# Sharing a spectrum product between three engines: ScalarE copies each spectrum out of PSUM, GpSimd forms one of the four products from the copy

## The chip, the cores and the metric

One Trainium2 chip, of which the kernel uses one core with its engines TensorE (PE), VectorE (DVE), ScalarE (ACT), GpSimd (POOL) and the queue of SyncE (SP) for transfers. The metric is the time of one launch in device microseconds; the median of three runs is taken.

## What is computed

The reference is one inference step through two trunk layers of a hybrid model: layer 0 has windowed attention beside a Hyena convolution, layer 1 a gated DeltaNet beside neighbourhood attention, and each layer ends with an expert-choice SwiGLU network. The change is in the Hyena part of layer 0, for the 1024 sample tokens (the 128 prompt tokens go through the same stage and are not touched by it):

```python
def hyena_mixer(z, conv_w, conv_b, w1, b1, w2, b2, w3, freq, skip):
    ...
    v, x1, x2 = jnp.split(zf, 3, axis=-1)
    filt = hyena_filter_bank(L, w1, b1, w2, b2, w3, freq)
    ...
    def long_conv(u, o):
        y = jnp.fft.irfft(jnp.fft.rfft(u, n=2 * L, axis=1) * filt[None, :, o], n=2 * L, axis=1)[:, :L]
        return y + u * skip[o]

    y = x1 * long_conv(v, 0)
    y = x2 * long_conv(y, 1)
```

Each of 512 channels is convolved twice with a filter as long as the signal, in the frequency domain: a forward transform, a complex product with the filter's spectrum, an inverse transform.

## The kernel before

The program is a row of stages, each a `Stage` block with barriers at its ends; within a stage every engine has its own instruction list, and semaphores order them. The stage of the change is `hyena_signals`, called once, between the attention of layer 0 and its output projection. Nothing of a neighbouring stage overlaps it.

Work in it is cut into eight blocks, in this order: for each of the two convolution orders the sample's channels 0 to 255 and 256 to 511 (S0A, S0B, then S1A, S1B), each pair followed by the same halves of the prompt (P0A, P0B, P1A, P1B). A sample block has eight iterations (`ft`), one per pair of 128 frequencies and 128 channels; a prompt block has one. They are numbered through by `n`: 0 to 7 S0A, 8 to 15 S0B, 16 and 17 the prompt, 18 to 25 S1A, 26 to 33 S1B, 34 and 35 the prompt.

One sample iteration goes through these hands:

- TensorE, `forward` (L1629): eight matmuls, cosine and sine parts of two time phases, into one of two PSUM banks (`freq`). It waits until the products of iteration n - 2 have read that bank (`prod_done`).
- VectorE, `multiply` (L1743): four products of 128x512, the bank times four views of the filter's spectrum (`spec`, a ring of four buffers in SBUF, filled by SyncE's queue), into `prod`, a ring of two. `y` is the output's time phase, `k` real or imaginary; the two products of y = 1 come first. Then a sum over the input phases for y = 0 (L1748). The products of iteration n wait until GpSimd has finished iteration n - 2 (`y_done`).
- GpSimd: the same sum for y = 1 (L1813), which needs the first two products, then two operations that combine the sums into the spectrum `Y` (L1817), which need both sums.

After a block's eight iterations TensorE transforms back (`backward`, L1646), ScalarE takes the odd part out of PSUM with a scale (`take_odd`, L1695), and VectorE finishes each 128 channels with four operations (`convolve`: L1760 and L1761 from PSUM, L1763 and L1766 from SBUF, 1024 wide). VectorE also makes the even and odd parts of the next order's input (`fold`, L1725 and L1726, from SBUF alone), which TensorE turns (L1609) and ScalarE copies (L1686).

The order on each engine is written out by hand as a list of calls. TensorE runs, for instance, `forward(S0B, range(6, 8))`, then `backward(S0A, (0, 1))`, then the prompt's forward transforms, then `backward(S0B, (0,))`. So the inverse of S0A waits for the last forward transform of S0B, and that of S0B for `y_done` of all its iterations. SyncE's queue is in order too: the loads of the gate rows wait for `u_done` (L1766), and the spectrum loads behind them wait in line.

## Time and profile before

| what | value |
|---|---|
| median of three runs | 3908.98 us (3904.9 to 3911.44) |
| the profiled execution | 3899.8 us, its span 3898.0 us |
| busy in the whole span | PE 86%, DVE 60%, ACT 44%, POOL 17% |
| mean granted TensorE clock | 0.926 |
| products of this stage, first and last start | 730.6 to 885.8 us |

The span is the time from the first to the last instruction of the profiled execution; its own time has some 2 us around it. Busy shares are averages over very different stages, and the stage of the change is about a twentieth of the span, so only rows cut to that stage say what waits there. The page's chain of what ended last covers only the final norm, at the very end of the program, and does not reach back to this stage.

### The profile page before, as it was taken

Reading aid. Unit: us, or ns where it says so; the run is one execution under the profiler, and the core shown is the slowest. Engines: PE = TensorE matmul, PEld = TensorE weight load, DVE = VectorE, ACT = ScalarE, POOL = GpSimd, SP = SyncE. Lnnn points to the kernel's source line nnn. Section 1 sums busy time; section 2 is a strip of 40 time slices with the busy share of each in tenths; the row PEclk is TensorE's granted clock in tenths of the full one; section 3 lists DMA queues with packets and bytes.
Section 4 is the critical chain, followed back from the end, with each engine's and each line's share of the span. In section 5 each row is a group of like instructions: output and inputs, shape, how many; then the busy total and the mean of one; then the engine's idle time right before and its main releaser. Section 6 shows DMA issues by size and latency. Waiting matters only on the chain. (4 is left out here: it accounts for less than half of the span.)

```text
span 3898.0 us, 60341 instructions
## 1 busy us (share of the span) xinstructions
PE 3349.1 (86%) x24369; PEld 2499.5 (64%) x24369; DVE 2319.3 (60%) x3530; ACT 1731.1 (44%) x2640; POOL 663.9 (17%) x544
## 2 busy tenths in 40 slices
PE   5979969677869999999699965877869599999994
PEld 1459945466646666666599954656757366666663
DVE  5253333685578888887521443535663778788884
ACT  2131145212346556666311134657853365666653
POOL 0011041342100000000110001507831000110000
PEclk8989989888979999999899987988979799999997
DMA  4143187425448888888344238117444578888875
GB/s 174 81 155 98 57 272 232 135 92 176 160 172 289 288 293 292 291 288 287 127 132 126 74 115 287 30 45 235 141 151 141 186 288 291 294 289 284 282 280 203
DMA packets 364075, 763.50 MB, mean 196 GB/s; under 512 B 88616, under 2 KB 204888, under 8 KB 361609
## 3 DMA queue, kind: packets, MB, share of 16 engines
q1 hardware_dynamic: 343530, 699.73, 50.7%
q0 software_dynamic: 17648, 59.50, 6.3%
q8 instruction: 193, 3.16, 0.3%
q10 hardware_dynamic: 2618, 0.40, 0.1%
q14 instruction: 86, 0.70, 0.1%
HBM read 640.89 MB, written 119.29 MB: 195 GB/s over the span
## 5 line engine op out<-in xcount | busy, mean ns | idle before, releaser
L2599 DVE TENSOR_TENSOR moe_w_low<-ffn_w,moe_w_high 128x1024 fp32r<-128x1024 f32 x768 | 900.3, 1220 | 90.0 <-ACT moe_w_high L2524 83.5
L2524 ACT ACTIVATE moe_w_high<-ffn_w 128x1024 fp32r<-128x1024 f32 x768 | 780.5, 1054 | 202.8 <-DMA ffn_w<-moe_w_gate 115.1
L2450 PE MATMUL moe_small<-ffn_w,ffn_xpT 128*16 128x512 f32 x2048 | 238.3, 594 | 0.0
L2428 PE MATMUL moe_G<-moe_w_high,moe_xT_high 128*128 128x512 f32 x512 | 185.3, 443 | 17.0 <-DVE moe_xT_low L2562 10.3
L2376 POOL DMA_INDIRECT scratch_x<-moe_ys,keep_slot_s x32 | 50.6, 1581 | 865.0 <-DVE moe_ys L2591 865.0
L224 PE MATMUL proj_mm<-proj_hT_low,proj_w_high 128*128 128x384 f32 x576 | 193.2, 335 | 0.0
L224 PE MATMUL proj_mm<-proj_hT_high,proj_w_low 128*128 128x384 f32 x576 | 193.1, 335 | 0.0
L224 PE MATMUL proj_mm<-proj_hT_high,proj_w_high 128*128 128x384 f32 x576 | 193.1, 335 | 0.0
L224 PE MATMUL proj_mm<-proj_w_high,proj_hT_high 128*128 128x416 f32 (+1 forms) x504 | 178.1, 353 | 12.0 <-POOL proj_hT_low L344 8.3
L224 PE MATMUL proj_mm<-proj_w_high,proj_hT_low 128*128 128x416 f32 (+1 forms) x504 | 176.8, 351 | 0.0
L224 PE MATMUL proj_mm<-proj_w_low,proj_hT_high 128*128 128x416 f32 (+1 forms) x504 | 175.8, 349 | 0.0
L2428 PE MATMUL moe_Y<-moe_w_high,moe_hT_high 128*128 128x512 f32 x512 | 166.6, 407 | 0.0
L2552 DVE TENSOR_SCALAR moe_xT<-moe_turn,keep_coef 128x128 f32<-128x128 f32 x248 | 84.7, 404 | 135.1 <-PE moe_turn L2404 135.1
L2428 PE MATMUL moe_G<-moe_w_low,moe_xT_high 128*128 128x512 f32 x512 | 161.9, 398 | 0.0
L2428 PE MATMUL moe_U<-moe_w_high,moe_xT_high 128*128 128x512 f32 x512 | 160.2, 394 | 0.0
L2428 PE MATMUL moe_G<-moe_w_high,moe_xT_low 128*128 128x512 f32 x512 | 160.0, 394 | 0.0
L2428 PE MATMUL moe_U<-moe_w_low,moe_xT_high 128*128 128x512 f32 x512 | 159.7, 393 | 0.0
L2428 PE MATMUL moe_Y<-moe_w_low,moe_hT_high 128*128 128x512 f32 x512 | 159.4, 392 | 0.0
L2428 PE MATMUL moe_Y<-moe_w_high,moe_hT_low 128*128 128x512 f32 x512 | 158.7, 391 | 0.0
L2428 PE MATMUL moe_U<-moe_w_high,moe_xT_low 128*128 128x512 f32 x512 | 158.6, 391 | 0.0
L451 ACT ACTIVATE proj_z<-proj_mm 128x384 f32<-128x384 f32 (+1 forms) x96 | 37.0, 412 | 263.6 <-PE proj_mm L224 259.7
L466 DVE CAST proj_w_high<-proj_w_raw 128x768 fp32r<-128x768 f32 (+1 forms) x60 | 34.0, 567 | 200.7 <-PE proj_mm L224 157.0
(500 smaller groups left out, 7138.4 us busy)
## 6 DMA issues: line engine op xcount, KB each, us to landing
ffn_w<-moe_w_gate SPq DMA_DIRECT2D x256, 512.0 KB, 6.0
ffn_w<-moe_w_up SPq DMA_DIRECT2D x256, 512.0 KB, 6.9
ffn_w<-moe_w_down SPq DMA_DIRECT2D x256, 512.0 KB, 5.3
attnrun_m_w<-w_ada SPq DMA_DIRECT2D x40, 1024.0 KB
scratch_spec<-front_room SPq DMA_DIRECT2D x8, 1536.0 KB, 5.1
scratch_conv<-proj_zf POOLq DMA_DIRECT2D x24, 512.0 KB, 2.9
hyena_spec<-scratch_spec SPq DMA_DIRECT2D x32, 384.0 KB, 3.5
scratch_tm<-proj_tm SPq DMA_DIRECT2D x45, 208.0 KB, 2.0
```

Of the source, the lines that this page charges most:

```text
L224: mm = nc.tensor.matmul(out, lhs(a, k), rhs(b, k), start=first and n == 0, stop=last and n == len(passes) - 1)
L451: ins = nc.scalar.activation(z[c % 2][:, lo + to:hi + to], banks[n % 6][:, lo - g * TG:hi - g * TG], ACT.Copy)
L466: nc.vector.tensor_copy(high, raw).then_inc(w_up, 1)
L2376: nc.gpsimd.indirect_dma_start(out=io["x"][l], out_offset=bass.IndirectOffsetOnAxis(ap=rows, axis=0), in_=src[e % 2][:], in_offset=None, c ...
L2428: mm = nc.tensor.matmul(bank[:, half, :], stat[a][:, k, :], cut[b][:, half * BANK:(half + 1) * BANK], start=k == 0 and i == 0, stop=k == K ...
L2450: nc.tensor.matmul(out, stat, w, start=k == 0, stop=k == KD - 1, tile_position=(0, 32 * q)).then_inc(small_done, 1)
L2524: nc.scalar.activation(w_high[n % CUT_ROOM][:], raw_rows(wall, n), ACT.Copy).then_inc(w_up, 1)
L2552: ins = nc.vector.tensor_scalar(xT[:, k, :], turned(k, e), co[:, 0, k:k + 1], co[:, 1, k:k + 1], ALU.mult, ALU.add)
L2599: nc.vector.tensor_tensor(w_low[n % CUT_ROOM][:], raw_rows(wall, n), w_high[n % CUT_ROOM][:].bitcast(F32), ALU.subtract).then_inc(w_cut, 1)
```

## The change

In the sample's iterations the fourth product (y = 1, k = 1) moves from VectorE to GpSimd. GpSimd does not read the PSUM bank itself: ScalarE first copies the bank's 128x512 to `side`, a new ring of two buffers in SBUF. GpSimd then multiplies the copy with the spectrum ahead of its sum. New waits: ScalarE's copy waits for the transform (`dft_done`) and for the side buffer (`crossed`, two iterations back); VectorE's products wait for the copy (`copied`); GpSimd's product waits for the copy and for the spectrum's load, its sum for its own product; and the spectrum loads wait for GpSimd's product four iterations back as well. On ScalarE the copies stand in the list where TensorE's forward transforms stand in its own.

```diff
@@ -1486,6 +1486,7 @@
         bwd_p = s.sb("bwd_p", [P, 2, 64])
         spec = [s.sb(f"spec{i}", [P, 2 * 3 * P]) for i in range(SPECS)]
         prod = s.sb("prod", [P, 2, 2, 2, 2, 2, P])
+        side = [s.sb(f"side{i}", [P, 2, HC]) for i in range(2)]
         odd = s.sb("odd", [P, 2, TS // 2])
         conv = s.sb("conv", [P, TS])
         skip = s.sb("skip", [P, 2, NCH])
@@ -1494,7 +1495,7 @@
         time_banks = [s.ps(f"time{i}", [P, 2, BANK]) for i in range(2)]
         u_in = [[s.sem(f"u_in{i}{h}") for h in range(2)] for i in range(2)]
         fwd_in, fwd_p_in, bwd_in = [s.sem(f"fwd_in{f}") for f in range(4)], s.sem("fwd_p_in"), s.sem("bwd_in")
-        summed, odd_summed = s.sem("summed"), s.sem("odd_summed")
+        summed, odd_summed, copied, crossed = s.sem("summed"), s.sem("odd_summed"), s.sem("copied"), s.sem("crossed")
         spec_in = [s.sem(f"spec_in{i}") for i in range(SPECS)]
         gate_in = [s.sem(f"gate_in{i}") for i in range(2)]
         folded, turned, turn_taken, dft_done, prod_done, y_done, inv_done, odd_done, conv_done, u_done = (
@@ -1514,6 +1515,10 @@
 
             return sum(g.ft for g, _, _ in blocks[:b] if g.i == 0)
 
+        def copies(n):
+
+            return sum(1 for b, (g, _, _) in enumerate(blocks) for m in range(freq0[b], freq0[b + 1]) if g.i == 0 and m < n)
+
         def channels(b):
             return (2 * blocks[b][2], 2 * blocks[b][2] + 1)
 
@@ -1535,6 +1540,7 @@
                     n = freq0[b] + f
                     if n >= SPECS:
                         sp.wait_ge(prod_done, 2 * (n - SPECS + 1))
+                        sp.wait_ge(crossed, copies(n - SPECS + 1))
                     if g.i == 0:
                         sp.dma_start(spec[n % SPECS][:], io["spec"][f // 2, o, :, 2 * h + f % 2].rearrange("p s v c -> p (s v c)")).then_inc(spec_in[n % SPECS], 16)
                     else:
@@ -1685,6 +1691,15 @@
                     act.wait_ge(turned, n + 1)
                     nc.scalar.activation(eoT_of[g.i][0:g.rows, t, part, h * HC:(h + 1) * HC], turn_banks[n % 2][0:g.rows, 0:HC], ACT.Copy).then_inc(turn_taken, 1)
 
+            def copy(b, fs):
+                for f in fs:
+                    n = freq0[b] + f
+                    c = copies(n)
+                    act.wait_ge(dft_done, n + 1)
+                    if c >= 2:
+                        act.wait_ge(crossed, c - 1)
+                    nc.scalar.activation(side[c % 2][:], freq_banks[n % 2][:], ACT.Copy).then_inc(copied, 1)
+
             def take_odd(b, js):
                 g, o, _ = blocks[b]
                 for j in js:
@@ -1695,18 +1710,26 @@
                     nc.scalar.activation(odd[:, i % 2, 0:g.half], time_banks[i % 2][:, 1, 0:g.half], ACT.Copy, scale=keep.tap_scale[:, g.i, at:at + 1]).then_inc(odd_done, 1)
 
             take_turned(S0A)
+            copy(S0A, range(0, 6))
             take_turned(S0B)
+            copy(S0A, range(6, 8))
+            copy(S0B, range(0, 6))
             take_turned(P0A)
             take_turned(P0B)
+            copy(S0B, range(6, 8))
             take_odd(S0A, (0, 1))
             take_odd(S0B, (0,))
             take_turned(S1A)
             take_odd(S0B, (1,))
+            copy(S1A, range(0, 6))
             take_turned(S1B)
+            copy(S1A, range(6, 8))
             take_odd(P0A, (0, 1))
             take_odd(P0B, (0, 1))
+            copy(S1B, range(0, 6))
             take_turned(P1A)
             take_turned(P1B)
+            copy(S1B, range(6, 8))
             for b in (S1A, S1B, P1A, P1B):
                 take_odd(b, (0, 1))
 
@@ -1730,6 +1753,7 @@
                 for f in fs:
                     n = freq0[b] + f
                     dve.wait_ge(dft_done, n + 1)
+                    dve.wait_ge(copied, copies(n + 1))
                     dve.wait_ge(spec_in[n % SPECS], 16 * (n // SPECS + 1))
                     if n >= 2:
                         dve.wait_ge(y_done, 2 * (n - 1))
@@ -1739,7 +1763,7 @@
                             nc.vector.tensor_tensor(both(n % 2)[:, k], freq_banks[n % 2][:], two(n % SPECS)[:, order, :], ALU.mult).then_inc(prod_done, 1)
                         continue
                     for y in (1, 0):
-                        for k, order in enumerate(orders):
+                        for k, order in enumerate(orders[0:2 - y]):
                             ins = nc.vector.tensor_tensor(prod[:, n % 2, y, k].rearrange("p s r c -> p s (r c)"), freq_banks[n % 2][:],
                                                           three(n % SPECS)[:, order, 1 - y:3 - y, :].rearrange("p s v c -> p s (v c)"), ALU.mult)
                         ins.then_inc(prod_done, 1)
@@ -1808,6 +1832,12 @@
                             nc.gpsimd.tensor_tensor(Y_of[1][:, f, k, 0, half], both(n % 2)[:, k, 0, :], both(n % 2)[:, k, 1, :], op).then_inc(y_done, 1)
                         continue
                     chunk = slice(h * HC + f % 2 * P, h * HC + f % 2 * P + P)
+                    c = copies(n)
+                    pool.wait_ge(copied, c + 1)
+                    pool.wait_ge(spec_in[n % SPECS], 16 * (n // SPECS + 1))
+                    nc.gpsimd.tensor_tensor(prod[:, n % 2, 1, 1].rearrange("p s r c -> p s (r c)"), side[c % 2][:],
+                                            three(n % SPECS)[:, ::-1, 0:2, :].rearrange("p s v c -> p s (v c)"), ALU.mult).then_inc(crossed, 1)
+                    pool.wait_ge(crossed, c + 1)
                     pool.wait_ge(prod_done, 2 * n + 1)
                     a = prod[:, n % 2, 1].rearrange("p k s r c -> p (k s) r c")
                     nc.gpsimd.tensor_tensor(a[:, :, 0, :], a[:, :, 0, :], a[:, :, 1, :], ALU.add).then_inc(odd_summed, 1)
```

How the instructions stand on GpSimd at the start of S0A; `hyena_side` is the copy. Before:

```order
L1813 TENSOR_TENSOR hyena_prod<-hyena_prod 128x4x128
L1817 TENSOR_TENSOR hyena_Y<-hyena_prod 128x2x128 x2
L1813 TENSOR_TENSOR hyena_prod<-hyena_prod 128x4x128
L1817 TENSOR_TENSOR hyena_Y<-hyena_prod 128x2x128 x2
L1813 TENSOR_TENSOR hyena_prod<-hyena_prod 128x4x128
L1817 TENSOR_TENSOR hyena_Y<-hyena_prod 128x2x128 x2
```

Now:

```order
L1838 TENSOR_TENSOR hyena_prod<-hyena_side,hyena_spec 128x512
L1843 TENSOR_TENSOR hyena_prod<-hyena_prod 128x4x128
L1847 TENSOR_TENSOR hyena_Y<-hyena_prod 128x2x128 x2
L1838 TENSOR_TENSOR hyena_prod<-hyena_side,hyena_spec 128x512
L1843 TENSOR_TENSOR hyena_prod<-hyena_prod 128x4x128
L1847 TENSOR_TENSOR hyena_Y<-hyena_prod 128x2x128 x2
```

Each sample iteration has four operations instead of three, the new one first; all 32 read this way.

VectorE, from the first products of S0A on, with the prompt's folds behind the second iteration. Before:

```order
L1743 TENSOR_TENSOR hyena_prod<-hyena_freq,hyena_spec 128x512 x4
L1748 TENSOR_TENSOR hyena_prod<-hyena_prod 128x4x128
L1743 TENSOR_TENSOR hyena_prod<-hyena_freq,hyena_spec 128x512 x4
L1748 TENSOR_TENSOR hyena_prod<-hyena_prod 128x4x128
L1725 TENSOR_TENSOR hyena_eo_prompt<-hyena_u_prompt 128x64
L1726 TENSOR_TENSOR hyena_eo_prompt<-hyena_u_prompt 128x64
```

Now:

```order
L1767 TENSOR_TENSOR hyena_prod<-hyena_freq,hyena_spec 128x512 x3
L1772 TENSOR_TENSOR hyena_prod<-hyena_prod 128x4x128
L1767 TENSOR_TENSOR hyena_prod<-hyena_freq,hyena_spec 128x512 x3
L1772 TENSOR_TENSOR hyena_prod<-hyena_prod 128x4x128
L1748 TENSOR_TENSOR hyena_eo_prompt<-hyena_u_prompt 128x64
L1749 TENSOR_TENSOR hyena_eo_prompt<-hyena_u_prompt 128x64
```

Three products stand where four stood, and nothing else on this engine has moved.

ScalarE, from the stage's start through S1A. Before:

```order
L1686 ACTIVATE hyena_eoT<-hyena_turn 128x256 x16
L1686 ACTIVATE hyena_eoT_prompt<-hyena_turn 64x256 x4
L1695 ACTIVATE hyena_odd<-hyena_time,keep_tap_scale 128x512 x3
L1686 ACTIVATE hyena_eoT<-hyena_turn 128x256 x8
L1695 ACTIVATE hyena_odd<-hyena_time,keep_tap_scale 128x512
```

Now:

```order
L1692 ACTIVATE hyena_eoT<-hyena_turn 128x256 x8
L1701 ACTIVATE hyena_side<-hyena_freq 128x512 x6
L1692 ACTIVATE hyena_eoT<-hyena_turn 128x256 x8
L1701 ACTIVATE hyena_side<-hyena_freq 128x512 x8
L1692 ACTIVATE hyena_eoT_prompt<-hyena_turn 64x256 x4
L1701 ACTIVATE hyena_side<-hyena_freq 128x512 x2
L1710 ACTIVATE hyena_odd<-hyena_time,keep_tap_scale 128x512 x3
L1692 ACTIVATE hyena_eoT<-hyena_turn 128x256 x8
L1710 ACTIVATE hyena_odd<-hyena_time,keep_tap_scale 128x512
L1701 ACTIVATE hyena_side<-hyena_freq 128x512 x6
```

The copies stand between the copies of turned tiles and the odd parts, in the places that the forward transforms have on TensorE.

## Rows read from the trace of the kernel before

**Rows 1.** Busy time by stretch: busy us (x instructions) of each engine, granted TensorE clock
```profile
727.00:786.50 59.50, 44.19 (x180) 33.93 (x181) 54.71 (x89) 3.93 (x12) 40.91 (x46) 0.92 0.49 142
820.90:888.00 67.10, 48.47 (x182) 38.62 (x183) 62.74 (x108) 5.18 (x16) 42.27 (x47) 0.80 0.31 97
...
742.00:746.00 4.00, 4.00 (x10) 3.15 (x11) 3.96 (x7) 0.00 (x0) 2.75 (x4) 0.50 0.49 106
```

**Rows 2.** Instructions of the product tile: ns min/median/max, first and last start
```profile
L1743 DVE TENSOR_TENSOR hyena_prod<-hyena_freq,hyena_spec x128: 672/676/692, 730.6 to 885.8; 128x512 f32<-128x512 f32 x128
L1817 POOL TENSOR_TENSOR hyena_Y<-hyena_prod x64: 717/727/1168, 733.9 to 888.2; 128x256 f32<-128x256 f32 x64
L1813 POOL TENSOR_TENSOR hyena_prod<-hyena_prod x32: 1262/1267/1282, 731.9 to 885.6; 128x512 f32<-128x512 f32 x32
L1748 DVE TENSOR_TENSOR hyena_prod<-hyena_prod x32: 691/900/920, 733.1 to 886.5; 128x512 f32<-128x512 f32 x32
```

**Rows 3.** Timeline, one iteration: start, us, engine, line, out<-in, count, [idle before <-releaser]
```profile
759.63 2.47 DVE L1743 TENSOR_TENSOR hyena_prod<-hyena_freq,hyena_spec 128x512 f32<-128x512 f32 x4
759.85 1.41 POOL L1817 TENSOR_TENSOR hyena_Y<-hyena_prod 128x256 f32<-128x256 f32 x2 [0.69 <-DVE hyena_prod L1748]
761.22 1.26 POOL L1813 TENSOR_TENSOR hyena_prod<-hyena_prod 128x512 f32<-128x512 f32 x1
762.13 0.90 DVE L1748 TENSOR_TENSOR hyena_prod<-hyena_prod 128x512 f32<-128x512 f32 x1
762.15 1.99 PE L1629 MATMUL hyena_freq<-hyena_eoT,hyena_fwd 128*128 128x256 f32 x8 [1.33 <-DVE hyena_prod L1743]
762.96 2.47 DVE L1743 TENSOR_TENSOR hyena_prod<-hyena_freq,hyena_spec 128x512 f32<-128x512 f32 x4
```

**Rows 4.** Timeline, the first product and the prompt's folds
```profile
730.57 2.48 DVE L1743 TENSOR_TENSOR hyena_prod<-hyena_freq,hyena_spec 128x512 f32<-128x512 f32 x4 [3.34 <-PE hyena_freq L1629]
...
737.26 1.40 POOL L1817 TENSOR_TENSOR hyena_Y<-hyena_prod 128x256 f32<-128x256 f32 x2 [0.69 <-DVE hyena_prod L1748]
737.31 0.75 DVE L1725 TENSOR_TENSOR hyena_eo_prompt<-hyena_u_prompt 128x64 f32<-128x64 f32 x1
...
738.66 0.21 DVE L1725 TENSOR_TENSOR hyena_eo_prompt<-hyena_u_prompt 128x64 f32<-128x64 f32 x1
```

**Rows 5.** Timeline, end of the first multiply stretch
```profile
780.63 13.98 PE L1646 MATMUL hyena_time<-hyena_bwd,hyena_Y 128*128 128x256 f32 x64
...
786.50 1.41 POOL L1817 TENSOR_TENSOR hyena_Y<-hyena_prod 128x256 f32<-128x256 f32 x2 [0.69 <-DVE hyena_prod L1748]
787.74 0.69 ACT L1695 ACTIVATE hyena_odd<-hyena_time,keep_tap_scale 128x512 f32<-128x512 f32 x1 [11.77 <-PE hyena_time L1646]
```

**Rows 6.** Timeline, start of the second stretch, with 512-wide folds
```profile
820.91 2.48 DVE L1743 TENSOR_TENSOR hyena_prod<-hyena_freq,hyena_spec 128x512 f32<-128x512 f32 x4
...
827.63 2.17 POOL L1817 TENSOR_TENSOR hyena_Y<-hyena_prod 128x256 f32<-128x256 f32 x2 [0.69 <-DVE hyena_prod L1748]
828.01 1.21 DVE L1726 TENSOR_TENSOR hyena_eo<-hyena_u 128x512 f32<-128x512 f32 x1
...
830.88 2.47 DVE L1743 TENSOR_TENSOR hyena_prod<-hyena_freq,hyena_spec 128x512 f32<-128x512 f32 x4
```

**Rows 7.** Timeline, the last prompt result before a load, and the product behind it
```profile
854.26 0.29 DVE L1766 TENSOR_TENSOR hyena_u_prompt<-hyena_conv,hyena_gate 128x128 f32<-128x128 f32 x1
...
858.86 2.48 DVE L1743 TENSOR_TENSOR hyena_prod<-hyena_freq,hyena_spec 128x512 f32<-128x512 f32 x4 [1.86 <-DMA hyena_spec<-scratch_spec]
```

**Rows 8.** Timeline, the inverse transforms of the second order
```profile
881.69 13.98 PE L1646 MATMUL hyena_time<-hyena_bwd,hyena_Y 128*128 128x256 f32 x64
...
897.51 14.08 PE L1646 MATMUL hyena_time<-hyena_bwd,hyena_Y 128*128 128x256 f32 x64
```

**Rows 9.** Timeline of GpSimd in another stage, a product and the sum behind it
```profile
2491.10 1.35 POOL L1043 TENSOR_TENSOR attn_E<-attn_Y,attn_M 128x495 f32<-128x495 f32 x1
2492.53 1.16 POOL L1045 TENSOR_TENSOR attn_Y<-attn_Y,attn_E 128x495 f32<-128x495 f32 x1
```

## The prediction

> **What bounds the kernel now.** The whole change lies in the convolution stage of layer 0, some 200 of the profiled 3898 us. The stages around it are separated by barriers, so what this stage gains or loses goes into the time one to one; what matters is which wait ends last inside it. I read the busy times by stretch first, then the instructions of the product tile, then the timeline.
>
> The two long multiply stretches are VectorE's: it is busy 54.71 of 59.50 us and 62.74 of 67.10 us, TensorE 44 and 48, GpSimd 41 and 42 [rows 1]. Call M the four products, A VectorE's own sum (L1748), O GpSimd's sum (L1813), Y its last two operations (L1817). From M to M is 3.33 us (759.63 to 762.96): M takes 2.47, A 0.90, with 0.04 of overlap. O starts after the second product, takes 1.26, then GpSimd waits 0.69 for A, and Y takes 1.41: 2.64 busy in each 3.33 [rows 3]. Between the stretches TensorE is the bound: the inverse transform of the first channel half runs 13.98 us without a gap [rows 5].
>
> **The change, part by part.** *VectorE* loses one product of four per iteration. Products come 0.60 us apart (four in 2.47, one lasts 0.68) [rows 2, 3], so M becomes 1.87 and M plus A about 2.6 to 2.8. If nothing else bound it, 32 iterations would give 19 us back.
>
> *ScalarE* gains 32 copies of 128x512 out of PSUM. The nearest row is its scaled copy of the same shape, 0.69 [rows 5]. It is idle most of the stretches (3.93 busy of 59.50 [rows 1]), and TensorE works two banks ahead, so this is hidden, except for the first of a run: about +0.75 before M(0) (730.57 [rows 4]).
>
> *GpSimd* gains the product C, 128x512 from two SBUF tensors. That shape costs it 1.267 as O [rows 2]; the bounds are 1.16 and 1.35, a sum and a product 495 wide in another stage [rows 9]. I take 1.27, the same size and stage. C to O and O to Y are now waits of GpSimd for itself; such a wait leaves 0.08 (2491.10 + 1.35 to 2492.53 [rows 9]). GpSimd's iteration is then 1.27 + 0.08 + 1.27 + 0.08 + 1.37 (Y until the next start: 759.85 to 761.22 [rows 3]) = 4.07 us. **GpSimd becomes the bound**: VectorE's 2.8 waits for it, because M(n) waits for Y(n-2).
>
> *The two engines in each other's way.* A reads two SBUF tensors, M reads PSUM and one. The rows tell them apart. M's 128 products span only 672 to 692 ns though GpSimd ran beside many of them. A lasts 0.69 alone and 0.90 when it starts 0.35 before O ends: it ends 0.55 after O [rows 2, 3]. A fold of 64 columns lasts 0.21 alone, 0.75 when it starts just after Y: it waits for the first Y to end [rows 4]. A fold of 512 columns lasts 1.21 and the Y pair beside it 2.17 instead of 1.41, and one Y takes at most 1168 instead of 727 ns: +0.44 [rows 2, 6]. So operations of these kinds take turns whole. At 4.07 us GpSimd would hardly be idle, so A in every iteration waits for GpSimd's current operation and then pushes the next back by 0.37 (0.44 less the 0.08 of the self-wait) to 0.44. I take 0.39: **an iteration is 4.46 us instead of 3.33.**
>
> The Trainium skill (SBUF — State Buffer, Who interferes with whom) says that a VectorE instruction with two SBUF inputs contends with a GpSimd one that reads SBUF, and that the later one blocks for the whole other instruction. That names the same pairs, but read literally the push-back is A's whole 0.69, the iteration 4.76, and the sum below some 6 us more; the rows' 0.44 is used. The Trainium skill (GPSIMD Engine Reference, Performance versus the Vector engine) give about 2.6 cycles per element at 1.2 GHz for a two-input operation, an estimate of 1.1 us for C before dispatch; with that the iteration would be 0.17 shorter and the sum some 4 us less. No run here shows C yet.
>
> Now the chain, iteration numbers 0 to 15 in the first half, 18 to 33 in the second (16, 17, 34, 35 are the prompt's and keep their form).
>
> *First stretch.* M(0) at 731.3. Iterations 0 to 4 start unevenly: GpSimd waits for A(0) as before, and the eight prompt folds after A(1) (0.21 each when free [rows 4]) take turns with O(1), both Y and C(2), so M(2) starts at 742.6. Following the turns, Y(4) ends at 756.1; from there 4.46 each: Y(11) ends at 756.1 + 7 x 4.46 = 787.3. M(13) can then start; it ends at 787.3 + 0.15 + 1.87 = 789.3; the last forward transform waits for it and takes 1.99 [rows 3]: the inverse starts at 791.3. Before: 780.63 [rows 5]. **+10.7.** (Before, this point hung on M(13), 14 rounds of VectorE; now on 12 of GpSimd.)
>
> *Is Y(15) hidden?* Before it ended at 787.91 [rows 5], some 8.6 us before the second half's inverse could start (15.8 after the first's, as 881.69 to 897.51 [rows 8]). Now: Y(14) 800.7, then 4.07 and two push-backs of about 1.05 by the convolution's two 1024-wide SBUF operations: 806.9. TensorE wants it at 791.3 + 15.8 = 807.1. Just hidden; all 8.6 of cover is gone, and from here each 0.1 us more per iteration costs 1.6 instead of 1.2.
>
> *Second stretch.* TensorE's part between is unchanged, so the old 820.91 for M(18) [rows 6] becomes 831.6; C(18) lies between the last two 1024-wide operations of VectorE and may hold the second up for 1.2: 832.8. M(19), four 512-wide folds in turn with O, Y, Y, C, and M(20) at 844.7, against 830.88: +13.8. The rest of the eight goes on at up to 4.46, and A(25) ends at 865.8. The prompt's convolutions follow, and their SBUF operations again take turns with C, O, Y: the one that ended at 854.55 (it releases the gate and, behind it in the same queue, the load that M(26) waits for 4.3 us later [rows 7]) ends at 870.6, so M(26) starts at 874.9 against 858.86: +16.0. M(26) to M(31) has eight more prompt folds in turns: M(31) ends 896.9, the inverse starts 898.9 against 881.69 [rows 8]: **+17.2.** Y(33), with the same two push-backs, ends at 914.5, wanted at 898.9 + 15.8 = 914.7: again just hidden. After it no C is left, and the end of the stage is as before.
>
> Sum: **+17.3 us**: 3899.8 + 17.3 = 3917.1 for the profiled execution, which stands 9.2 under the median of the three timed; the median goes to 3908.98 + 17.3 = 3926.3. Elsewhere nothing is touched, so 0 there.
>
> *Bounds.* About 22 GpSimd iterations lie on this chain. C from 1.16 to 1.35: -2.4 to +1.8. Push-back from 0.2 (A meets a gap each second time) to 0.69: -4.2 to +6.6.
>
> **The rivals.**
>
> *1. No blocking: the change about even.* If GpSimd and A run freely beside each other, the iteration is 4.07 and the folds are free. First inverse at 784.3 (+3.7); but the second stretch, with its folds and prompt convolutions, never lets GpSimd become the bound for long, VectorE saves 0.6 a round, and the last inverse would start at about 878.7, 3.0 earlier than now. Time 3906. It decides from a push-back near zero. Against it: every row of [rows 3, 4, 6]. 8%.
>
> *2. Blocking as seen, but half of it absorbed.* If A, delayed, slips into the self-waits and Y's gaps, an iteration is 4.2 to 4.3: +8 to +12, 3917 to 3921. 17%.
>
> *3. A full turn, and the tail takes over.* If each A costs GpSimd A's whole 0.69 [rows 2], an iteration is 4.76. Y(15) then ends at 756.6 + 10 x 4.76 + 4.07 + 2.1 = 810.4, after TensorE is free for it (793.9 + 15.8 = 809.7), so the inverse itself waits for GpSimd: +13.9 against the 796.5 of before. The way to M(31) adds the 6.5 of above and 9 x 0.3, the last Y about 0.5: +23.6, 3932.6. With two operations held up per iteration, 4.9 us, the same sum gives +27, 3936. For it: A will meet a busy GpSimd every time. Against it: the 0.44 of [rows 2]. 14%. This is the case that the Trainium skill's rule above, read literally, stands for.
>
> *4. TensorE's clock.* TensorE, busy 1.99 in 3.33 now, would be busy 1.99 in 4.46, with 2.5 idle. The level does fall in this stage: 0.50 from 742 to 746, ten matmuls in 4 us, right after TensorE had waited for the prompt folds; the mean is 0.92 in the first stretch and 0.80 in the second [rows 1]. At that level (1.2 GHz) a forward transform of eight takes some 3.2, hidden inside an iteration except the last one before each inverse, and each inverse starts slow: 2 to 3 us twice, +22, 3931. 13%.
>
> *5. Faster.* C or O much cheaper than 1.27 and no blocking. 3%.
>
> **How the numbers follow.** A measurement of this kernel can tell about 0.2%, 7.8 us, from no change. The forecast (+14 to +21 around 3926) has 45%, rivals 2, 3, 4 together 44%, 1 and 5 11%. The range 3917 to 3937 takes in rivals 2 and 4 and most of 3, and leaves out 1, 5 and what goes beyond 3. Slower by more than 0.2%: 45 + 27 + most of rival 2 = 0.86; within: rival 1 and the light end of 2, 0.11; faster 0.03.
>
> **What would show it.** C near 1.27 us, 32 times. O and Y otherwise as now, but some of them 0.4 longer. A (now 0.69 to 0.92) up to 1.7. GpSimd busy above 90% of the multiply stretches (69% and 63% now), VectorE's long idle waits released by Y, ScalarE's copy about 0.7 and never the last releaser but once or twice. First inverse 10 to 11 us later, last 17. Wrong if iterations run at 4.1 or less, if A stays at 0.7 to 0.9 beside a busy GpSimd, or if the prompt convolutions do not lengthen: then the second stretch gives back what the first costs.

## The result, and the profile after

The changed kernel takes **3916.83 us**, the median of 7 runs (3912.32 to 3923.43), against 3904.9 (7 runs, 3899.36 to 3911.44) of the kernel before on the same chip: **ratio 1.0027 [1.0018, 1.0037]**, which is 10.5 us more [7.0, 14.4]; the two medians are 11.9 apart. The forecast was 3926.3 with a range of 3917 to 3937. The direction was right, and the measured time lies 0.17 us below the low end. The profiled execution took 3923.43 us (span 3921.5), that of before 3899.8 (span 3898.0). It was forecast at 3917.1, and only 14.4 of the 23.6 us between these two lie in the stage of the change.

The convolution stage can be read more finely than the whole kernel, whose single executions scatter by some 5 us (standard deviation over all its runs). From the start of its first fold (VectorE's even and odd parts of the input) to the end of its last prompt result it takes 203.1 us before and **217.5 after, +14.4**, where the forecast was +17.3.

The letters are the prediction's: M the products on VectorE, A VectorE's sum, O GpSimd's sum, Y its two last operations, C its new product; M(n) is M of iteration n. The product tile after, as [rows 2] before: ns min/median/max, first and last start. L1838 is C, L1772 is A.

```profile
L1767 DVE TENSOR_TENSOR hyena_prod<-hyena_freq,hyena_spec x96: 673/680/694, 727.0 to 899.3; 128x512 f32<-128x512 f32 x96
L1847 POOL TENSOR_TENSOR hyena_Y<-hyena_prod x64: 718/728/1588, 730.3 to 907.4; 128x256 f32<-128x256 f32 x64
L1838 POOL TENSOR_TENSOR hyena_prod<-hyena_side,hyena_spec x32: 1258/1270/2189, 727.0 to 902.3; 128x512 f32<-128x512 f32 x32
L1843 POOL TENSOR_TENSOR hyena_prod<-hyena_prod x32: 1262/1270/2129, 728.4 to 903.7; 128x512 f32<-128x512 f32 x32
L1772 DVE TENSOR_TENSOR hyena_prod<-hyena_prod x32: 691/1075/1796, 729.0 to 900.0; 128x512 f32<-128x512 f32 x32
```

C costs what O costs, 1.27 us. M's products are as before, 673 to 694 ns. A's median went from 0.90 to 1.08 us, with the same work in it.

Busy time by stretch after (busy us and instructions of PE, PEld, DVE, ACT, POOL, then granted clock, DMA share, GB/s); the first two lines answer to [rows 1], the third is the steady part of the first:

```profile
724.00:793.50 69.50, 48.08 (x188) 36.78 (x189) 51.62 (x73) 14.11 (x30) 61.75 (x59) 0.88 0.41 117
828.00:901.00 73.00, 49.79 (x188) 40.05 (x189) 63.89 (x93) 13.87 (x31) 61.84 (x58) 0.81 0.29 89
753.00:793.00 40.00, 28.00 (x106) 21.35 (x107) 27.05 (x38) 6.28 (x14) 38.58 (x37) 0.87 0.32 94
```

and the same steady part of the kernel before:

```profile
753.00:786.50 33.50, 24.49 (x109) 18.89 (x108) 32.85 (x50) 1.29 (x4) 25.98 (x30) 1.00 0.44 136
```

GpSimd is busy 38.58 of 40.00 us (before 25.98 of 33.50), VectorE 27.05 of 40.00 (before 32.85 of 33.50). Over the two whole stretches GpSimd is busy 89% and 85%, not above 90% as the prediction's sign had it. One iteration after, from the timeline, as [rows 3] before:

```profile
759.93 1.27 POOL L1838 TENSOR_TENSOR hyena_prod<-hyena_side,hyena_spec 128x512 f32<-128x512 f32 x1
760.10 1.89 DVE L1767 TENSOR_TENSOR hyena_prod<-hyena_freq,hyena_spec 128x512 f32<-128x512 f32 x3 [1.40 <-POOL hyena_Y L1847]
...
761.28 1.27 POOL L1843 TENSOR_TENSOR hyena_prod<-hyena_prod 128x512 f32<-128x512 f32 x1
761.31 0.60 ACT L1701 ACTIVATE hyena_side<-hyena_freq 128x512 f32<-128x512 f32 x1 [3.81 <-PE hyena_freq L1635]
762.02 1.07 DVE L1772 TENSOR_TENSOR hyena_prod<-hyena_prod 128x512 f32<-128x512 f32 x1
...
762.63 1.74 POOL L1847 TENSOR_TENSOR hyena_Y<-hyena_prod 128x256 f32<-128x256 f32 x2
764.32 1.26 POOL L1838 TENSOR_TENSOR hyena_prod<-hyena_side,hyena_spec 128x512 f32<-128x512 f32 x1
```

Read it from GpSimd's side: C, O, Y, C follow each other, and the only idle time is the 0.08 us between an operation and the next one that needs its result. Y takes 1.74 where it took 1.41. VectorE idles 1.40 until the Y of two iterations earlier frees the products' tile. From C to C is 4.39 (before 3.33 from M to M).

The two ends of the first half, as [rows 5] and [rows 8] before:

```profile
785.82 13.98 PE L1652 MATMUL hyena_time<-hyena_bwd,hyena_Y 128*128 128x256 f32 x64
...
798.63 2.27 POOL L1847 TENSOR_TENSOR hyena_Y<-hyena_prod 128x256 f32<-128x256 f32 x2
...
801.65 0.94 PEld L1652 LDWEIGHTS hyena_time<-hyena_bwd,hyena_Y 128*128 128x128 f32 x5 [0.33 <-issue]
```

Y(15) ends at 800.90; TensorE comes for it at 801.65 and has not waited for it. Times from the first fold's start (719.38 before, 716.69 after), and what the forecast moved them by:

| | before | after | moved | forecast |
|---|---|---|---|---|
| M(0) | 11.19 | 10.34 | -0.8 | +0.75 |
| first inverse | 61.25 | 69.13 | +7.9 | +10.7 |
| M(18) | 101.5 | 111.5 | +10.0 | +11.9 |
| M(20) | 111.5 | 123.0 | +11.5 | +13.8 |
| M(26) | 139.5 | 152.4 | +13.0 | +16.0 |
| second inverse (the second order's first) | 162.31 | 176.56 | +14.3 | +17.2 |

### The profile page after: what moved, and what is told of

Its sections match the earlier page's. It is cut to its first block and busy times, and to the rows that moved or that the text cites. A ratio compares the mean times of both kernels' runs of the same rounds, so it can differ in the third digit from the quotient of the medians.

```text
span 3921.5 us, 60524 instructions
## 1 busy us (share of the span) xinstructions
PE 3364.5 (86%) x24369; PEld 2511.2 (64%) x24369; DVE 2318.4 (59%) x3498; ACT 1749.3 (45%) x2672; POOL 719.7 (18%) x576
## 5 line engine op out<-in xcount | busy, mean ns | idle before, releaser
L958 ACT ACTIVATE attnrun_pT<-attnrun_pt 128x512 f32<-128x512 f32 (+4 forms) x144 | 89.4, 621 | 148.0 <-PE attnrun_pt L738 147.2
```

The costliest lines, as they stand in the source:

```text
L958: nc.scalar.activation(pT[:, u % 4, 0:n], pt[u % RT][:, 0:n], ACT.Copy).then_inc(pT_done, 1)
```

## The experiments

Each kernel was timed beside the kernel before on one chip, in five rounds. "Stage" is the length above, read from one profiled execution of each kernel; up to 1.7 us of it depend on TensorE's clock in the first transforms (last section). Ratios are to the kernel before.

**Controls.** The kernel before once more, and the changed kernel twice more, unedited.

> The kernel before, unchanged, timed against itself. Its stage, from the first fold's start to the last result's end, was 203.1 us in the first trace. If the stage's length is set by its chain, it is 202 to 205 again and the ratio is 1.000 within 0.001. If single executions of the stage differ by several microseconds (the clock level at the first forward transform, say), the length here shows it: then part of the +14.4 us seen between the two first traces is chance.

> The changed kernel, unchanged. Theory: its stage is 14 us longer than before (217.5 us in the first trace) and all of it goes into the time: ratio 1.0036. Rival: something outside the stage gives part of it back, ratio 1.0027 or less, as first timed (+10.6 us), with the stage again at 217.

> The changed kernel once more. Stage: 217.5 us if TensorE's first forward transforms run at the full clock as in both executions seen so far (3.72 us for sixteen), 219 if they run at half for the first ten (5.25 us), as in those of the kernel before. Ratio 1.0036 if the stage's +14.2 us is all there is; both earlier intervals, 1.0018 to 1.0037 and 1.0027 to 1.0054, hold it.

The control: 0.9994 [0.9985, 1.0004], stage 203.6. The changed kernel: 1.0040 [1.0027, 1.0054] and 1.0043 [1.0028, 1.0057], stages 217.5 and 217.9. The three intervals of the changed kernel share 1.0028 to 1.0037; the stage's 14.4 us are 0.37% of 3904.9. The 51 runs of the kernel before that stood beside these three have a median of 3905.9, the 19 of the changed one 3920.3: +14.4.

**VectorE's sum away from the changed kernel** (it leaves out the sum of the cosine products; O still runs).

```diff
-                    dve.wait_ge(prod_done, 2 * n + 2)
-                    a = prod[:, n % 2, 0].rearrange("p k s r c -> p (k s) r c")
-                    nc.vector.tensor_tensor(a[:, :, 0, :], a[:, :, 0, :], a[:, :, 1, :], ALU.add).then_inc(summed, 1)
...
-                    pool.wait_ge(summed, sums(b) + f + 1)
+                    pool.wait_ge(prod_done, 2 * n + 2)
```

> The changed kernel with VectorE's sum for y = 0 left out, so that VectorE has no instruction with two SBUF inputs beside GpSimd in the iterations. Theory of turns: GpSimd still bounds, its iteration falls from 4.39 to about 4.05 us, no Y lasts longer than 0.73 in the steady run; the stage is about 5 to 7 us shorter than with the change (211 to 213 us). Rival, GpSimd's own four operations and their waits already take 4.39: the iteration stays at 4.39 and the stage at 217.

Ratio 1.0008 [0.9997, 1.0019], stage 207.8. Its timeline:

```profile
768.25 1.27 POOL L1835 TENSOR_TENSOR hyena_prod<-hyena_side,hyena_spec 128x512 f32<-128x512 f32 x1
...
769.60 1.27 POOL L1840 TENSOR_TENSOR hyena_prod<-hyena_prod 128x512 f32<-128x512 f32 x1
...
770.95 1.41 POOL L1844 TENSOR_TENSOR hyena_Y<-hyena_prod 128x256 f32<-128x256 f32 x2
772.31 1.27 POOL L1835 TENSOR_TENSOR hyena_prod<-hyena_side,hyena_spec 128x512 f32<-128x512 f32 x1
```

It is 4.06 from C to C (the forecast's own sum was 4.07), and Y is back at 1.41. So GpSimd's work is 4.06 of the 4.39, and the other 0.33 is what A pushes it back. The stage is 9.7 us shorter than with A, below the 211 to 213 expected; M(0) came 1.5 us later here, with TensorE's clock low in the first transforms, so that from M(0) on it is 11.2.

**GpSimd's product added, nothing taken from VectorE** (kernel before; GpSimd multiplies a constant tile by the same spectrum into a tile that nobody reads).

```diff
+            nc.gpsimd.memset(side[:], 1.0).then_inc(side_set, 1)
...
+                    c = copies(n)
+                    pool.wait_ge(dft_done, n + 1)
+                    pool.wait_ge(spec_in[n % SPECS], 16 * (n // SPECS + 1))
+                    nc.gpsimd.tensor_tensor(spill[:].rearrange("p s c -> p s c"), side[:],
+                                            three(n % SPECS)[:, ::-1, 0:2, :].rearrange("p s v c -> p s (v c)"), ALU.mult).then_inc(crossed, 1)
+                    pool.wait_ge(crossed, c + 1)
```

> The kernel before with only GpSimd's share added: it forms one product more from two SBUF tensors, into a tile that nobody reads, while VectorE keeps all four and ScalarE copies nothing. Theory: GpSimd bounds and VectorE's relief is worth nothing: iteration 4.39 us, stage within 2 us of the changed kernel's 217.5, ratio about 1.003 to 1.004. Rival, VectorE's relief still counts in the folds, the prompt and the ends of the blocks: the stage is 4 us or more longer than the changed kernel's, above 221.

Ratio 1.0053 [1.0034, 1.0071], stage 223.3, 5.8 more than the change: the expectation (within 2 us of it) missed, its rival held. An iteration takes 4.61:

```profile
765.26 1.27 POOL L1822 TENSOR_TENSOR hyena_spill<-hyena_side,hyena_spec 128x512 f32<-128x512 f32 x1
765.43 2.49 DVE L1749 TENSOR_TENSOR hyena_prod<-hyena_freq,hyena_spec 128x512 f32<-128x512 f32 x4 [1.40 <-POOL hyena_Y L1831]
766.61 1.26 POOL L1827 TENSOR_TENSOR hyena_prod<-hyena_prod 128x512 f32<-128x512 f32 x1
767.95 1.97 POOL L1831 TENSOR_TENSOR hyena_Y<-hyena_prod 128x256 f32<-128x256 f32 x2
767.96 0.69 DVE L1754 TENSOR_TENSOR hyena_prod<-hyena_prod 128x512 f32<-128x512 f32 x1
...
769.88 1.27 POOL L1822 TENSOR_TENSOR hyena_spill<-hyena_side,hyena_spec 128x512 f32<-128x512 f32 x1
```

With four products A comes just when Y does, goes first, and Y takes 0.56 more instead of 0.33. That is how a VectorE that is not the bound is still felt: a later A costs GpSimd more. Not all of the 5.8 is this. M(0) came 0.7 later, and around the first inverse TensorE ran at a lower clock, 2.82 and 14.88 us where the changed kernel has 1.99 and 13.98, 1.7 together:

```profile
786.42 2.82 PE L1635 MATMUL hyena_freq<-hyena_eoT,hyena_fwd 128*128 128x256 f32 x8 [2.45 <-DVE hyena_prod L1749]
789.04 14.88 PE L1652 MATMUL hyena_time<-hyena_bwd,hyena_Y 128*128 128x256 f32 x64
```

**VectorE's relief alone** (changed kernel without C; the fourth product is left out, its place holds a constant, ScalarE still copies).

```diff
-                        act.wait_ge(crossed, c - 1)
+                        act.wait_ge(copied, c - 1)
...
+            for i in range(2):
+                nc.gpsimd.memset(prod[:, i, 1, 1], 1.0).then_inc(crossed, 1)
...
-                    nc.gpsimd.tensor_tensor(prod[:, n % 2, 1, 1].rearrange("p s r c -> p s (r c)"), side[c % 2][:],
-                                            three(n % SPECS)[:, ::-1, 0:2, :].rearrange("p s v c -> p s (v c)"), ALU.mult).then_inc(crossed, 1)
-                    pool.wait_ge(crossed, c + 1)
```

> The changed kernel with GpSimd's product left out (its place in the product tile is set once, at the stage's start): VectorE forms three products, ScalarE copies, nobody forms the fourth. It shows what VectorE's relief would be worth for free. Theory: VectorE bounds again, M and its sum take 1.87 + 0.7 to 0.9, iteration 2.65 to 2.8 us against 3.33, the stage about 15 to 17 us shorter than before (187 us), ratio 0.996. Rival, the copy in the chain (VectorE waits for it) or GpSimd's 2.64 plus waits hold the iteration at 3.0 or more: under 8 us gained.

Ratio 0.9988 [0.9976, 1.0000], stage 199.0: 4.1 us less than before, not 15 to 17. An iteration still takes 3.33, with three products:

```profile
766.81 1.87 DVE L1766 TENSOR_TENSOR hyena_prod<-hyena_freq,hyena_spec 128x512 f32<-128x512 f32 x3
767.03 1.41 POOL L1843 TENSOR_TENSOR hyena_Y<-hyena_prod 128x256 f32<-128x256 f32 x2 [0.69 <-DVE hyena_prod L1771]
...
768.40 1.27 POOL L1839 TENSOR_TENSOR hyena_prod<-hyena_prod 128x512 f32<-128x512 f32 x1
768.72 1.50 DVE L1771 TENSOR_TENSOR hyena_prod<-hyena_prod 128x512 f32<-128x512 f32 x1
...
770.14 0.68 DVE L1766 TENSOR_TENSOR hyena_prod<-hyena_freq,hyena_spec 128x512 f32<-128x512 f32 x1
```

A took up what M gave back: it starts 0.60 earlier and lasts 1.50 instead of 0.90, and ends 0.55 after O as before. The row shows it as busy; alone it lasts 0.69. So a new theory was needed for the 3.33, a **loop of turns**. A can't finish before O is over and ends 0.55 behind it. Y waits for A and starts 0.15 later. The next O starts 1.37 after Y and lasts 1.26. 0.55 + 0.15 + 1.37 + 1.26 = 3.33, with no term of VectorE's products in it.

**Three kernels for that loop.** The kernel before without A (it leaves out the cosine sum, with the edit shown above); the kernel before with three product tiles in the ring instead of two:

```diff
-        prod = s.sb("prod", [P, 2, 2, 2, 2, 2, P])
+        prod = s.sb("prod", [P, 3, 2, 2, 2, 2, P])
...
-                    if n >= 2:
-                        dve.wait_ge(y_done, 2 * (n - 1))
+                    if n >= 3:
+                        dve.wait_ge(y_done, 2 * (n - 2))
```

and the kernel before with the cosine products and A first, O waiting for the sine products:

```diff
-                    for y in (1, 0):
+                    a = prod[:, n % 2, 0].rearrange("p k s r c -> p (k s) r c")
+                    for y in (0, 1):
...
-                    dve.wait_ge(prod_done, 2 * n + 2)
-                    a = prod[:, n % 2, 0].rearrange("p k s r c -> p (k s) r c")
-                    nc.vector.tensor_tensor(a[:, :, 0, :], a[:, :, 0, :], a[:, :, 1, :], ALU.add).then_inc(summed, 1)
+                        if y == 0:
+                            dve.wait_ge(prod_done, 2 * n + 1)
+                            nc.vector.tensor_tensor(a[:, :, 0, :], a[:, :, 0, :], a[:, :, 1, :], ALU.add).then_inc(summed, 1)
...
-                    pool.wait_ge(prod_done, 2 * n + 1)
+                    pool.wait_ge(prod_done, 2 * n + 2)
```

The diffs show the lines that matter; with three tiles every `n % 2` of the product tile becomes `n % 3`.

> The kernel before with VectorE's sum for y = 0 left out, four products kept. Loop theory: without A there is no turn to wait for; GpSimd bounds with 1.27 + 0.08 + 1.37 = 2.72, iteration 2.72 us. Rival, VectorE's work counts: 3.33 less A's 0.90 = 2.43. The stage is 8 to 12 us shorter than before either way (191 to 195 us).

> The kernel before with the product tile a ring of three instead of two, nothing else. Loop theory: the loop A, Y, O, A runs through one iteration's own operations, not through the ring, so the iteration stays 3.33 us, the stage 203, ratio 1.000. Rival: the ring of two is what holds VectorE to GpSimd; then the iteration falls to 3.05 to 3.15 and the stage to 198.

> The kernel before with one thing reordered on VectorE: the y = 0 products first, its sum A right behind them, the y = 1 products last; GpSimd's O waits for the latter. New theory, from the run with the product left out, whose iteration stayed at 3.33 us with three products: 3.33 is no sum of VectorE's work but a loop of turns, A to Y (0.15), Y (1.37), O (1.26), A behind O (0.55). With A no longer right behind O the loop opens: GpSimd needs 2.64 plus one push-back of 0.44, VectorE 2.40 plus 0.65, iteration 3.05 to 3.15, stage about 3 to 6 us shorter than before (197 to 200 us), ratio 0.999. Rival, VectorE's busy sum is the bound as I predicted: four products and one sum are still there, iteration 3.3, stage 203.

Without A: 0.9964 [0.9952, 0.9976], stage 191.0, and GpSimd runs O, Y, O without a gap, 2.72 an iteration:

```profile
754.33 1.27 POOL L1810 TENSOR_TENSOR hyena_prod<-hyena_prod 128x512 f32<-128x512 f32 x1
...
755.68 1.42 POOL L1814 TENSOR_TENSOR hyena_Y<-hyena_prod 128x256 f32<-128x256 f32 x2
757.05 1.27 POOL L1810 TENSOR_TENSOR hyena_prod<-hyena_prod 128x512 f32<-128x512 f32 x1
```

If VectorE's four products had been the bound, it would have been 2.43. Three tiles: 0.9997 [0.9986, 1.0008], iterations 3.33 to 3.34, so the ring isn't it:

```profile
756.42 2.47 DVE L1743 TENSOR_TENSOR hyena_prod<-hyena_freq,hyena_spec 128x512 f32<-128x512 f32 x4
758.92 0.91 DVE L1748 TENSOR_TENSOR hyena_prod<-hyena_prod 128x512 f32<-128x512 f32 x1
759.75 2.47 DVE L1743 TENSOR_TENSOR hyena_prod<-hyena_freq,hyena_spec 128x512 f32<-128x512 f32 x4
```

Its stage is 201.7, 1.4 shorter than before: M(6) and M(24) follow after 3.34, where in the kernel before they took 4.17 and 4.40 (M(6) had waited 0.76 for TensorE there). Sum first: 1.0018 [1.0007, 1.0029], stage 212.1; from O to O it is 3.12 and 3.91 by turns. That expectation (3.05 to 3.15 each time, stage 197 to 200) missed. That with O starting later the ring of two binds every other time is borne out by the next kernel.

**Both together**, in the kernel before, and three tiles in the changed kernel, and the sum first in the changed kernel.

> The reordering of VectorE (A behind its own pair, y = 1 products last) with the ring of three. With two it alternated 3.12 and 3.91. If the 3.91 came from the ring of two (the product waiting for Y with 0.20 idle, A then behind O again), every iteration is now 3.05 to 3.15, the stage 196 to 200, ratio 0.998 to 0.999, faster than both kernels. Rival: A falls behind O every second time whatever the ring; stage 210 or more.

> The changed kernel with the ring of three. GpSimd bounds, so its iteration stays 4.39 us in the steady run; stage within 2 us of 217.5, ratio 1.0036. Rival: the changed kernel is late because VectorE starts each M only when Y ends; if that matters the iteration falls to 4.07 and the stage to 210.

> The changed kernel with the same reordering on VectorE: y = 0 products, A, then its one y = 1 product. GpSimd's four operations (4.07) and one push-back bound it either way: iteration 4.39 to 4.52, stage 216 to 220, ratio 1.0035. Rival, A's place decides the push-back: if A falls beside a self-wait twice, the iteration is 4.3 or less and the stage 215 or less.

Sum first with three tiles: 1.0006 [0.9995, 1.0017], no faster, where 0.998 to 0.999 was expected. The loop is open all the same, 3.12 from M to M in the steady part, with VectorE never idle:

```profile
759.00 2.47 DVE L1744 TENSOR_TENSOR hyena_prod<-hyena_freq,hyena_spec 128x512 f32<-128x512 f32 x4
...
761.50 0.69 DVE L1749 TENSOR_TENSOR hyena_prod<-hyena_prod 128x512 f32<-128x512 f32 x1
761.71 1.75 POOL L1818 TENSOR_TENSOR hyena_Y<-hyena_prod 128x256 f32<-128x256 f32 x2
762.11 1.28 DVE L1744 TENSOR_TENSOR hyena_prod<-hyena_freq,hyena_spec 128x512 f32<-128x512 f32 x2
```

A lasts 0.69 there, but the stage is 208.6, longer than before and than the 196 to 200 expected. The gain of 0.2 an iteration is lost elsewhere: the iterations with folds take 6.4 to 7.7 (before 5.5 to 6.8), the second one behind them 3.8 to 4.0 (before 3.3), and the way from the first inverse to M(18) is 1.4 longer. The changed kernel with three tiles: 1.0033 [1.0020, 1.0046], 4.51 an iteration, stage 218.7, of which 1.5 is a later M(0) at TensorE's lower clock; A falls beside C there, and C lasts 1.73. With the sum first: 1.0064 [1.0048, 1.0080], 4.39, stage 222.2 (216 to 220 was expected). More room for VectorE doesn't help while GpSimd is the bound; it only lets A fall elsewhere.

**Parts of the change.** The copies and VectorE's wait for them alone, in the kernel before; in the changed kernel, the product moved by half (256 columns on GpSimd, 256 on VectorE), and moved in every fourth iteration only.

```diff
+                    act.wait_ge(dft_done, n + 1)
+                    if c >= 2:
+                        act.wait_ge(copied, c - 1)
+                    nc.scalar.activation(side[c % 2][:], freq_banks[n % 2][:], ACT.Copy).then_inc(copied, 1)
...
+                    dve.wait_ge(copied, copies(n + 1))
```

> The kernel before with ScalarE's copies and VectorE's wait for them alone; VectorE keeps four products and GpSimd gets none. Theory: hidden except for the first of each run, stage +0.5 to +3 us, ratio 1.000 to 1.001. Rival: each product run now starts 0.6 us later whenever TensorE is just in time, stage +8 us or more.

> Half of the fourth product (the sine half, 256 columns) on GpSimd, the other half on VectorE, ScalarE copies 256 columns. Theory: GpSimd's product falls from 1.27 to 0.73, its iteration from 4.39 to about 3.85; VectorE's M is 2.2. GpSimd still bounds. The stage is about 208 us, 5 above before and 9 below the change; ratio 1.001. Rival, the delay of the change comes from the extra semaphore hops and turns, not from the product's length: the stage is above 213.

> The product moves to GpSimd only in iterations 3 and 7 of each eight. GpSimd needs 2.64 + 0.35 of every other iteration, so the one long iteration in four is taken up by its slack. Theory: mean GpSimd need (3 x 3.0 + 4.39) / 4 = 3.35, VectorE's mean (3 x 3.33 + 2.8) / 4 = 3.2: stage within 2 us of before, 201 to 205, ratio 1.000. Rival: the long iteration cannot be absorbed, since VectorE may run only two products ahead: stage 206 or more.

Copies alone: 1.0007 [0.9997, 1.0017], no change that can be measured; its iterations are 3.33. Its one profile has a stage of 209.2, 6.1 more than before where 0.5 to 3 was expected. Of this, 0.8 lies ahead of M(0), 1.6 at M(5) and M(6), which waited 0.35 and 2.19 for a copy behind a late transform, and 2.5 between M(16) and M(18), with TensorE at a lower clock between the stretches (0.74 from 807 to 820 against 1.00 in before):

```profile
807.00:820.00 13.00, 10.58 (x40) 8.05 (x40) 5.99 (x7) 3.65 (x9) 1.01 (x1) 0.74 0.13 47
```

The ratio gives only 2.7 us, so these 6 us may belong in part to that one execution; why the clock was lower stays open. Half moved: 1.0036 [1.0023, 1.0049], stage 211.5, 3.97 an iteration (208 and 3.85 were expected); A falls on the second operation of Y there and costs it 0.44. Its time rose by more than its stage (8.4 us, 0.22%), which stays open too. Every fourth: 1.0015 [1.0005, 1.0026], stage 204.5; its time is longer than before by a little, while the stage's 1.4 us are no more than what the kernel with three tiles fell short by, with the same iterations as before. So the cost grows with the share that is moved. No kernel that computes everything beat the kernel before.

## Why the prediction was right in kind and wrong in size

**Right: GpSimd becomes the bound.** C is 1.27, the iteration without A 4.06 (4.07 forecast), with A 4.39 (4.46), A lasts up to 1.80 (1.7), GpSimd is busy 96% of the steady part. A push-back of 0.33 was measured, 0.39 was taken.

What the prediction lacked is what a turn costs, and the rows give it. An A that is held ends 0.54 to 0.55 after the GpSimd operation ahead of it, in every row, whether it lasted 0.90 or 1.80. The operation of Y that is held ends 0.58 to 0.59 after A, a C or an O 1.12 to 1.14 after. Alone they last 0.69, 0.73 and 1.27, so each can spend its first 0.14 or so while the other still runs, and then waits for the whole rest. The push-back is therefore the time from Y's start to A's end, less 0.14: 763.10 - 762.63 - 0.14 = 0.33 in the changed kernel, 768.65 - 767.95 - 0.14 = 0.56 with the product added. The 0.44 of [rows 2], from which 0.39 was taken, is one case among these.

The Trainium skill (SBUF — State Buffer, Who interferes with whom) says that the one that comes second fully blocks while the first has the shared ports. The trace agrees, on the pairs and on the blocking: no held operation ended sooner than these times after the first. What it doesn't bear out is the prediction's reading that A's whole 0.69 would then be lost; that is more than the second one still has to wait. The Trainium skill (GPSIMD Engine Reference, Performance versus the Vector engine) gave an estimate of 1.1 us for C before dispatch; the trace has 1.27 with it, as the row of O had.

**Right: the cover of Y(15) and Y(33).** Both ends were forecast as just hidden, and they are: 800.90 against 801.65, and 908.14 (905.87 + 2.27) against 909.08. The second half's inverse starts 15.83 after the first's both times, as forecast.

**Mis-sized: the first stretch, the term +10.7, which measured +7.9.** Of the 2.8, *1.6 are M(0)*, forecast 0.75 later and found 0.8 earlier. The term itself was near: the copy takes 0.60, and M(0) starts 0.69 after it does (726.34 to 727.03). What was not in the sum is TensorE ahead of it: M(0) needs the first eight matmuls, and these took 3.56 before (727.01 to 730.57) and 2.03 after (724.31 to 726.34), 1.53 less. The timeline, kernel before, then after:

```profile
727.01 5.25 PE L1629 MATMUL hyena_freq<-hyena_eoT,hyena_fwd 128*128 128x256 f32 x16 [0.47 <-ACT hyena_eoT L1686]
```
```profile
724.31 3.72 PE L1635 MATMUL hyena_freq<-hyena_eoT,hyena_fwd 128*128 128x256 f32 x16 [0.47 <-ACT hyena_eoT L1692]
```

The same sixteen matmuls start 7.6 us after the first fold in both. They take 5.25 where the first seven (not ten, as one expectation has it) follow each other at half clock (0.43 apart instead of 0.22), and 3.72 at full clock. At equal clock the change would have cost some 16 us of the stage, an estimate from 14.4 and this 1.5. The other 1.2 are the fold turns before M(2), 10.7 for 11.3 from M(0), and the way from there to the inverse, 48.1 for 48.7, mostly the 0.07 less per iteration.

**Right in sum, by other terms: the way from there to the second inverse**, +6.4 for +6.5. C(18) did hold up the convolution's last 1024-wide operation:

```profile
824.90 2.19 POOL L1838 TENSOR_TENSOR hyena_prod<-hyena_side,hyena_spec 128x512 f32<-128x512 f32 x1 [15.21 <-issue]
...
826.00 2.17 DVE L1790 TENSOR_TENSOR hyena_u<-hyena_conv,hyena_gate 128x1024 f32<-128x1024 f32 x1
```

by 0.94 (2.17 for the 1.23 that it takes elsewhere), not 1.2. But M(18) came 2.1 later than the first inverse, not 1.2: the rest is TensorE at a lower clock (0.94 from 801 to 829, against 1.00 from 797 to 821 before), where the turns and the half inverse between take 1.2 longer together (7.62 for 7.07 in the latter). That is rival 4, small and in another place than named; where the prediction named it, at the last transform before the inverse and in the inverse itself, it showed in the kernel with the product added (1.7 us), not here. The way on to M(26) cost 3.0 (forecast 4.1); the prompt's convolutions take turns as forecast (three of the eight L1790 of the prompt last 0.69, 1.31 and 0.70 where a free one takes 0.29). Not as forecast: ScalarE's copy was the last releaser of VectorE's products five times, with 4.7 us of idle time, instead of once or twice.

**The step that put the time outside the range is the anchor, together with the mis-sized first stretch.** The measured time is 9.5 us below the forecast: 3.1 are the anchor, 2.9 the sum (+17.3 for +14.4, nearly all of it the first stretch's 2.8), and 3.5 the luck of the seven runs. The sum was added to 3908.98, the median of three runs, though the profiled execution stood 9.2 lower. Over 51 runs the kernel before has 3905.9. From there, +17.3 is 3923.2 and +14.4 is 3920.3, which is what the 19 runs of the changed kernel give and lies within the range; the 7 runs of the result happened to lie 3.5 lower. The low end, 3917.0, rested on rival 2 above the high anchor; with 3905.9 it would have been 3914.

**A wrong reading that the sum didn't need: "if nothing else bound it, 32 iterations would give 19 us back".** What bounds isn't VectorE's 3.37 us of busy time, which is 0.90 of A with 0.21 of waiting in it; it is the loop of turns O, A, Y. Taking a fourth of M away shortened nothing (3.33), taking A away gave 2.72 (GpSimd's own work). So the change's gain was never 19 us: alone it is worth 4.1 us of the stage. This is shown by VectorE's relief alone, by the kernel without A, and by three tiles; the loop's opening is shown by sum first with three tiles. Beside a busy GpSimd the relief is worth 0.22 us an iteration in the steady part (4.61 against 4.39), by the moment at which A falls; of the 5.8 us between those two stages, some 2.4 are M(0) and the clock around the first inverse.

**The rivals.** 1 (no blocking) fell with every A of 1.08 and Y of 1.74. 2 (absorbed, 4.2 to 4.3 an iteration, +8 to +12) missed the iteration, 4.39; that the first seven runs gave a time near its 3917 is luck. 3 (full turn, 4.76) fell: the most that A cost a Y was 0.56. 4 is seen in small, above. The likeliest case held in its mechanism, GpSimd's iteration and the turns, with +14.4 at the low end of its own +14 to +21.

## What to carry to other kernels

An engine whose busy time fills the span need not be the bound: its instruction may be waiting, inside its own duration, for another engine's instruction to end. Compare an instruction's median with its minimum, and look for a loop of turns, before pricing a relief. Moving work from an engine at 0.68 us an operation to one at 1.27 paid nothing here, where the second engine had 0.69 us of idle time in each iteration; each VectorE operation with two SBUF inputs cost GpSimd a turn on top (0.33 to 0.56 us in the steady iterations). And put the forecast on many timed runs of a kernel, not on the median of three.

## What the runs showed of the hardware that I had not expected

- Waiting for a turn is recorded as busy time of the operation that waits: A is 0.69, 0.90, 1.07, 1.50 and 1.80 us long with the same work; a 64-wide fold of 0.21 lasted 1.30 beside C; C and O lasted 2.19 and 2.13 beside the 1024-wide operations.
- A turn costs the other engine less than the operation's length, for an A of 0.69: 0.33 (A begun 0.60 before Y's start, behind O), 0.46 (A begun 0.09 before C) and 0.56 (A begun with Y). In all of them the second operation ends at a fixed time after the first.
- The level of TensorE's clock in its first sixteen forward matmuls differs between kernels that are the same up to there: full (3.72 us) in the changed kernel's three executions and in its version with the sum first; half for the first five to eight (4.8 to 5.5 us) in the others, the changed kernel with three tiles (5.27) among them. I found nothing in the rows ahead of them that tells the two apart. It is worth 1.1 to 1.7 us of the stage here; its cause stays open.
- The granted clock fell to 0.87 in the steady part after, with TensorE busy 28.00 of 40.00 us, against 1.00 at 24.49 of 33.50 before; the longer transforms lie inside an iteration and cost nothing there.
